# Attention ends in another order, norm chains by halves, and merged products whose bank halves VectorE adds

## The chip, the cores and the metric

One Trainium2 chip; the program runs on 1 of its cores. The metric is the device time of one execution in microseconds (us), and the median of the runs shown is taken.

## What is computed

Two transformer blocks over 256 tokens of width 1024, in float32, as a chain of ten stages on one residual x:

```python
# layer 0: neighborhood attention; layer 1: differential attention
x = x + rms_norm(attention(rms_norm(x, g0)), g1)
x = x + rms_norm(conv_glu_ffn(rms_norm(x, g2)), g3)     # gelu(conv3(h@Wg)+b) * (h@Wv) @ Wo, inner width 2816
x = x + sigmoid(rms_norm(x, g4) @ Wgate) * (p @ Wproj)  # "ple"
# second block, once
h = h + 0.5 * (silu(n(h)@Wg) * (n(h)@Wu)) @ Wd          # "glu", inner width 2816
h = h + mixer(n(h))                                     # HGRN2 and causal attention
h = h + 0.5 * (silu(n(h)@Wg) * (n(h)@Wu)) @ Wd
h = h + sigmoid(n(h) @ Wgate) * (p @ Wproj)
return rms_norm(h)
```

## The kernel before

`PHASES` (stages 0 to 9) is na, ffn, ple, da, ffn, ple, glu, mix, glu, ple. x lies as two tiles of 128 tokens by 1024.

**Products in three parts.** Each float32 product is made of three TensorE matmuls in the reduced format fp32r (`product3`, L1419 to L1421): high part by high part, low by high, high by low, summed in PSUM. Every weight slab of 128 x 2048 values is loaded into `raw` (3 slots), ScalarE copies it into `w_hi` (L615), VectorE subtracts the copy into `w_lo` (L953); both have `RING` = 5 slots. `feed(upto)` on either engine works through the slabs in order up to that number, and waits until the slot's last reader is done. The activations lie transposed in `hT_hi` and `hT_lo`, two separate tiles of 8 x 256 columns.

**PSUM.** Four banks `acc` of 512 columns, and four banks `work`, used in turn: group g opens bank g % 4 when group g-4 has been read out.

**Feed-forward stages (`ffn`).** 22 tiles c of 128 inner channels. `up(c)`: gate product into columns 0 to 255 of one bank, value product into columns 256 to 511 of the same, 8 k-steps of three 256-wide matmuls each. VectorE runs the convolution (three instructions, ffn only), ScalarE the gelu or silu, VectorE multiplies by the value half (L1204), ScalarE makes the high part (L789), VectorE the low part (L1209). `down(c)`: 12 matmuls of 512 columns into `acc`. TensorE's order is up(c), down(c-1). Even tiles carry three slab conversions on both engines.

**Attention (`attention`).** TensorE runs 16 groups of columns, c.0 to c.15 (`half_columns`: 8 k-steps of three 256-wide matmuls), which give transposed queries and keys; ScalarE reads each bank out (`columns_out`). `gap(ph, n)` lists what runs behind group n: S u (scores of head pair u), T u (transposition of its weights), V u (values), O q (transposition of half of the output). S u stands at `SCORED[u]`; T u 2 groups later in stage 0 and 3 in stage 3; V u one more. VectorE's `scores` scales, adds the table (L1058) and takes the maximum (L1063); ScalarE's `exps` follows, then in stage 3 VectorE's `weights` (L1068 to L1077). `tail(ph)` orders the rest: P are pieces of the output projection's first half, K of its second half; K (t, half) ends `acc` bank 2t + half.

**Ends of stages (`end_of_acc`, the end of `ffn`).** For each token tile: ScalarE's square sum over 1024 columns (L619), on the row of GpSimd mean and power (L501, L502), VectorE's two instructions that scale by gain and add to x (L1019, L1023; `post`), a second square sum (`pre`), mean and power again, VectorE's scaling (L1009; `normed`), TensorE's transposition (L1464; `turn_x`), and the parts of hT (`tile_parts`, L985, L624, L964). Between these stands one `feed`.

Of the kernel before, what the change touches and what calls it, by code (L numbers as in the profile page):

```python
# [20 lines left out]
ALU = mybir.AluOpType  # L21
# [43 lines left out]
SCORED = [3, 4, 7, 8, 11, 12, 15]  # L65
# [12 lines left out]
def tail(ph):  # L78

    first = [] if ph == 0 else [("V", 5)]  # L80
    return first + [("P", (0, 0)), ("S", 7), ("P", (0, 1)), ("T", 6), ("P", (1, 0)), ("V", 6), ("T", 7),
                    ("P", (1, 1)), ("V", 7), ("O", 1), ("K", (0, 0)), ("K", (0, 1)), ("K", (1, 0)), ("K", (1, 1))]


def plan(w):
# [47 lines left out]
    def event(name, n, scale, squares):  # L133
        E[name] = (len(ev), cols[0])
        cols[0] += n
        cols[1] += squares
        ev.append((n, scale, cols[1]))
# [5 lines left out]
    for t in range(T):  # L143
        event(f"pre0.{t}", 1, 1.0 / D, 1)
    for ph, kind in enumerate(PHASES):
# [48 lines left out]
        elif kind in ("ffn", "glu"):  # L194
            norm_stage(ph, 1)
            stage(f"up{ph}", FT - 1)
            if PHASES[ph + 1] == "ple":
                stage(f"pT{ph + 1}", 1, 1)
            stage(f"last_up{ph}", 1)
# [6 lines left out]
            B[f"down{ph}"] = count["down"]  # L206
            for j in range(STEPS):
                add(a[:, a0 + j * FB:a0 + (j + 1) * FB].rearrange("(k p) n -> p k n", p=P), KT, FB, "used")
                t_slab(b, b0 + j * FB, G[f"up{ph}"] + 2 * j + 1 if j < STEPS - 1 else G[f"last_up{ph}"])
                count["down"] += 2  # L210
                add(c[j * FB:(j + 1) * FB, :].rearrange("(k p) n -> p k n", p=P), 2, D,
                    ("down", count["down"]))
# [47 lines left out]
        for name in {"na": ("post0", "pre0", "post1", "pre1"), "da": ("post0", "pre0", "post1", "pre1"),  # L260
                     "ffn": ("post0", "post1", "pre0", "pre1")}.get(kind, ("pre0", "pre1")):
            event(f"{name[:-1]}{ph if name[:4] == 'post' else ph + 1}.{name[-1]}", 1, 1.0 / D, 1)
# [3 lines left out]
def two_blocks(nc, w, out):  # L266
# [3 lines left out]
    with ctx:  # L270
# [17 lines left out]
        hT_hi = sb("hT_hi", [P, KT, S], F32R)  # L288
        hT_lo = sb("hT_lo", [P, KT, S], F32R)
# [37 lines left out]
        cbuf, glu, hid32 = z(0, 512, (2, S)), z(512, 1024, (2, S)), z(1024, 1536, (2, S))  # L327
        pp, prow = z(2048, 4096, (T, D)), z(4096, 4608, (T, 256))
# [18 lines left out]
        ebr = z(9216, 9728, None, 8)  # L347
        tT = sb("tT", [8, 32])
# [24 lines left out]
        conv_done, act_done = sem("conv_done"), sem("act_done")  # L373
        hid_hi_done, hid_ready, sig_done = sem("hid_hi_done"), sem("hid_ready"), sem("sig_done")
# [28 lines left out]
        def up_bank(ph, c):  # L403
            return G[f"up{ph}"] + c if c < FT - 1 else G[f"last_up{ph}"]
# [10 lines left out]
        def score_bank(u):  # L415
            return 2 * (u % 2) if u < 6 else 2
# [43 lines left out]
        def _(sp):  # L460
# [9 lines left out]
            for t in range(T):  # L470
                sp.wait_ge(out_ready, t + 1)
                sp.dma_start(out[0, t * P:(t + 1) * P, :], xn[:, t, :]).then_inc(stored, 16)
            sp.wait_ge(stored, 16 * T)
# [3 lines left out]
        def _(pool):  # L477
# [18 lines left out]
            def powers(name):  # L496
                while raised[0] <= names.index(name):
                    i, c = E[names[raised[0]]]
                    n, scale, squares = EV[i]
                    pool.wait_ge(sq_done, squares)  # L500
                    link(pool.tensor_scalar(ms[:, c:c + n], ssq[:, c:c + n], scale, EPS, ALU.mult, ALU.add))  # L501
# [39 lines left out]
            pool.wait_ge(x_ready, 2)  # L541
# [63 lines left out]
        def _(act):  # L605
# [30 lines left out]
            def pre(ph, t):  # L636
                if ph == 0:
                    act.wait_ge(x_loaded[t], 16)
                else:
                    act.wait_ge(x_ready, 2 * (ph - 1) + t + 1)  # L640
                square_sum(xn[:, t, :], x[:, t, :], E[f"pre{ph}.{t}"][1])

            def post(ph, t):
                if ph in ACC:
                    act.wait_ge(acc_full, ACC[ph] + 2 * t + 2)
                else:
                    act.wait_ge(down_done, B[f"down{ph}"] + FT - 1 + t)
                square_sum(xn[:, t, :].rearrange("p (a b) -> p a b", a=2), acc[:, 2 * t:2 * t + 2, :],
                           E[f"post{ph}.{t}"][1])

            def end_of_acc(ph, b, finish):
                feed(b + 5)
                finish(0)
                feed(b + 6)
                pre(ph + 1, 0)
                tile_parts(ph + 1, 0)
                finish(1)
                feed(b + 7)
                pre(ph + 1, 1)
# [50 lines left out]
            def columns_out(ph, n):  # L710
                g, f = G[f"c{ph}.{n}"], n // 4 * 2 + n % 2
                if n // 2 % 2 == 0:
                    evac(g, backwards(qT[:, f, :].rearrange("p (t c) -> p t c", t=T)),
                         bank(g)[:, 0:S].rearrange("p (t c) -> p t c", t=T))
                else:
                    evac(g, kT[:, f, :], bank(g)[:, 0:S])

            def attention(ph):
# [8 lines left out]
                for n in range(HALVES):  # L727
# [3 lines left out]
                    columns_out(ph, n)  # L731
# [11 lines left out]
                if ph == 3:  # L743
                    for u in after(ph, gap(ph, HALVES - 1), "V") + [5]:
                        head_squares(ph, u)
                unit_exps(ph, 6)
                feed(wo + 5)
                unit_exps(ph, 7)
                weights_turned(ph, 6)
                if ph == 3:  # L750
                    head_squares(ph, 6)
                weights_turned(ph, 7)
                if ph == 3:
                    head_squares(ph, 7)
                output_parts(ph, 1)
# [13 lines left out]
            def ffn(ph, kind):  # L769
                b, c0 = B[ph], B[f"down{ph}"]  # L770
                feed(b + 3)
                for c in range(FT):
# [8 lines left out]
                    else:  # L781
                        full(act, g)
# [1082 lines left out]
```

## Time and profile before

| | |
|---|---|
| median of 3 runs | 1406.74 us (1406.55 to 1407.74) |
| the profiled execution | 1408.87 us |
| its span, first to last instruction | 1407.3 us |
| granted clock, mean | 0.955 |
| PE, PEld, DVE, ACT, POOL busy | 90%, 81%, 59%, 45%, 8% |

PE are TensorE's matmuls, PEld its weight loads, DVE is VectorE, ACT ScalarE, POOL GpSimd. A granted clock of 1.00 is 2.4 GHz, 0.50 is 1.2 GHz. The ends of matmuls are modelled, so the pace of TensorE is read from the distance of starts, not from durations. Where matmul follows matmul closely the profile calls PE busy, whatever the pace. The stages take, by the writes of x: 0 to 188 us na, to 386 ffn, to 416 ple, to 583 da, to 780 ffn, to 819 ple, to 1011 glu, to 1178 mix, to 1373 glu, to the end ple.

### The profile page before, as it was taken

To read this page: it belongs to the slowest core of one execution; us is meant where nothing else is said; L and a number is where in the kernel's file an instruction comes from. 1 tells how busy PE (TensorE), PEld (TensorE's weight loads), DVE (VectorE), ACT (ScalarE), POOL (GpSimd) and SP (SyncE) were. 2 spreads that over 40 slices of the span, in tenths; PEclk is the share of its full clock that TensorE was granted. 3 is DMA by queue.
4 is the path that set the end of the run, shared out by engine and by line. 5 is a ranking of instruction groups with operands and counts; after the bars stand their busy time and mean duration, and the time that the engine had idled before them with its cause. 6 is when DMAs were issued, how large, how long until landed. Compare 5 with 4: busy or idle time off the path is not lost. (4 is left out here: it accounts for less than half of the span.)

```text
span 1407.3 us, 19395 instructions
## 1 busy us (share of the span) xinstructions
PE 1264.3 (90%) x8145; PEld 1144.0 (81%) x8145; DVE 826.4 (59%) x921; ACT 629.0 (45%) x854; POOL 108.2 (8%) x216
## 2 busy tenths in 40 slices
PE   6997769999999776699999979999889987999997
PEld 5887669999878764599998779999767776999995
DVE  6645346666776654566666845555456775444455
ACT  5634334444465552344444644434354643333444
POOL 4000030000010000100000100000015321000000
PEclk9999889999999989899999989999999998999999
DMA  9631155555447320265554525555243324655550
GB/s 287 210 115 63 58 158 180 180 180 180 180 165 233 115 73 30 86 203 192 191 188 151 187 90 182 188 193 193 84 149 113 131 72 149 202 180 180 180 176 35
DMA packets 148730, 214.62 MB, mean 153 GB/s; under 512 B 4378, under 2 KB 114396, under 8 KB 148644
## 3 DMA queue, kind: packets, MB, share of 16 engines
q1 hardware_dynamic: 145356, 205.62, 43.9%
q0 software_dynamic: 1632, 4.71, 1.3%
q10 hardware_dynamic: 1656, 3.05, 0.6%
q8 instruction: 65, 1.06, 0.3%
q14 instruction: 21, 0.17, 0.0%
HBM read 212.30 MB, written 1.06 MB: 152 GB/s over the span
## 5 line engine op out<-in xcount | busy, mean ns | idle before, releaser
L953 DVE TENSOR_TENSOR w_lo<-raw,w_hi 128x2048 fp32r<-128x2048 f32 (+1 forms) x195 | 445.1, 2289 | 213.2 <-PE work L1421 131.2
L1419 PE MATMUL work<-hT_hi,w_hi 128*128 128x256 f32 x1696 | 488.7, 288 | 11.1 <-DVE hT_lo L964 6.1
L1420 PE MATMUL work<-hT_lo,w_hi 128*128 128x256 f32 x1696 | 485.6, 286 | 0.0
L1421 PE MATMUL work<-hT_hi,w_lo 128*128 128x256 f32 x1696 | 485.3, 286 | 0.0
L615 ACT ACTIVATE w_hi<-raw 128x2048 fp32r<-128x2048 f32 (+1 forms) x195 | 368.3, 1894 | 10.8 <-DMA raw<-in_na_w_qkv 9.4
L1419 PEld LDWEIGHTS work<-hT_hi,w_hi 128*128 128x128 f32 x1696 | 331.6, 195 | 19.8 <-issue 16.7
L1420 PEld LDWEIGHTS work<-hT_lo,w_hi 128*128 128x128 f32 x1696 | 331.5, 195 | 3.1
L1421 PEld LDWEIGHTS work<-hT_hi,w_lo 128*128 128x128 f32 x1696 | 331.1, 195 | 0.0
L1419 PE MATMUL acc<-w_hi,aux_hi 128*128 128x512 f32 x384 | 151.6, 395 | 6.5 <-DVE aux_lo L1209 3.6
L1420 PE MATMUL acc<-w_lo,aux_hi 128*128 128x512 f32 x384 | 150.5, 392 | 0.0
L1421 PE MATMUL acc<-w_hi,aux_lo 128*128 128x512 f32 x384 | 149.5, 389 | 0.0
L780 ACT ACTIVATE Z<-Z 128x256 f32<-128x256 f32 x44 | 18.4, 418 | 199.3 <-DVE Z L1199 199.3
L501 POOL TENSOR_SCALAR ms<-ssq 128x1 f32<-128x1 f32 (+2 forms) x38 | 17.4, 458 | 1156.7 <-ACT xn L619 1022.6
L783 ACT ACTIVATE Z<-work 128x256 f32<-128x256 f32 x44 | 16.9, 384 | 194.4 <-PE work L1421 194.4
L1419 PEld LDWEIGHTS acc<-w_hi,aux_hi 128*128 128x128 f32 x384 | 72.4, 189 | 21.6 <-issue 6.9
L666 ACT ACTIVATE Z<-work 128x512 f32<-128x512 f32 (+3 forms) x98 | 48.5, 515 | 92.4 <-PE work L1421 76.2
L1196 DVE TENSOR_SCALAR Z<-work,convT 128x256 f32<-128x256 f32 x44 | 23.8, 541 | 107.3 <-PE work L1421 107.3
L1421 PEld LDWEIGHTS acc<-w_hi,aux_lo 128*128 128x128 f32 x384 | 72.1, 188 | 15.8
L1419 PE MATMUL acc<-w_hi,hT_hi 128*128 128x512 f32 x176 | 74.5, 423 | 8.2 <-DVE hT_lo L964 7.8
L1420 PEld LDWEIGHTS acc<-w_lo,aux_hi 128*128 128x128 f32 x384 | 72.5, 189 | 11.6
L1204 DVE TENSOR_TENSOR Z<-Z,work 128x256 f32<-128x256 f32 x88 | 36.7, 418 | 63.2 <-ACT Z L783 51.6
L1464 PE MATMUL work<-ident,xn 128*128 128x128 f32 x112 | 23.4, 376 | 54.9 <-DVE xn L1009 54.5
(201 smaller groups left out, 1421.5 us busy)
## 6 DMA issues: line engine op xcount, KB each, us to landing
raw<-in_ffn_w_in SPq DMA_DIRECT2D x44, 1024.0 KB, 5.7
raw<-in_ffn_w_out SPq DMA_DIRECT2D x22, 1024.0 KB, 5.0
raw<-in_w_gate SPq DMA_DIRECT2D x22, 1024.0 KB, 5.4
raw<-in_w_up SPq DMA_DIRECT2D x22, 1024.0 KB, 5.8
raw<-in_w_down SPq DMA_DIRECT2D x22, 1024.0 KB, 4.9
raw<-in_na_w_qkv SPq DMA_DIRECT2D x12, 1024.0 KB, 6.7
raw<-in_da_w_qkv SPq DMA_DIRECT2D x12, 1024.0 KB, 5.3
raw<-in_ple_w_gate SPq DMA_DIRECT2D x8, 1024.0 KB, 5.1
```

The lines of the kernel that those rows point to most:

```text
L501: link(pool.tensor_scalar(ms[:, c:c + n], ssq[:, c:c + n], scale, EPS, ALU.mult, ALU.add))
L615: act.activation(w_hi[:, n % RING, 0:size], raw[:, n % RAW, 0:size], ACT.Copy).then_inc(hi_done, 1)
L666: act.activation(dst, src, func).then_inc(bank_free[g % WORK], 1)
L780: act.activation(glu[:, c % 2, :], cbuf[:, c % 2, :], ACT.Gelu_apprx_tanh).then_inc(act_done, 1)
L783: act.activation(glu[:, c % 2, :], bank(g)[:, 0:S], ACT.Silu).then_inc(act_done, 1)
L953: dve.tensor_tensor(w_lo[:, n % RING, 0:size], raw[:, n % RAW, 0:size], w_hi[:, n % RING, 0:size].bitcast(F32), ALU.subtract).then_inc(lo_ ...
L1196: link(dve.tensor_scalar(dst, src[:, 0:S], tap[1], tap[3], ALU.mult, ALU.add))
L1204: dve.tensor_tensor(hid32[:, c % 2, :], glu[:, c % 2, :], bank(g)[:, S:2 * S], ALU.mult)\
L1419: pe.matmul(dst, stationary[0], moving[0], start=first, stop=False)
L1420: pe.matmul(dst, stationary[0], moving[1], start=False, stop=False)
L1421: return pe.matmul(dst, stationary[1], moving[0], start=False, stop=last)
L1464: ins = pe.transpose(b[:, cols(i)], v[:, t, cols(4 * q + i)], ident[:, :])
```

## The change

1. **Merged products.** `hT_hi` and `hT_lo` become halves of one tile `hT_both` [P, 8, 2, 256]. In `up` and `half_columns` a k-step is one 512-wide matmul (w_hi by both parts, into both halves of a bank) and one 256-wide (w_lo by the high part, into the first half). Gate and value get a bank each, so a tile takes two groups instead of one. VectorE adds the halves of each bank with a `tensor_reduce` of 512 columns into 256.
2. **In ffn and glu** the convolution and the silu read the sum in SBUF (`gsum`), the value's sum goes to `hid32`, and the product is made in place. In **attention** the read-out of c.n moves from ScalarE to VectorE, at the head of each turn n of its loop.
3. **Norm chains by halves.** Square sums over 512 columns, two for each tile; GpSimd makes two mean steps and one power; `post` multiplies `acc` by the gain without waiting for the power, then scales and adds to x, one half at a time; x_ready, out_ready and down_done count halves.
4. **Attention ends.** S 6 moves from group 15 to 14. `tail` moves V 7 and O 1 ahead of P (1, 1) in stage 0 and V 7 ahead of it in stage 3. The transposition of x's first tile moves behind K (1, 1). In `end_of_acc` VectorE's `normed` moves ahead of its `feed(b + 6)`, and `feed(b + 7)` behind all parts; `feed(wo + 6)` moves into the attention.

```diff
-SCORED = [3, 4, 7, 8, 11, 12, 15]
+SCORED = [3, 4, 7, 8, 11, 12, 14]
...
+    late = {0: [("S", 7), ("P", (0, 0)), ("T", 6), ("P", (0, 1)), ("V", 6), ("T", 7), ("P", (1, 0)), ("V", 7), ("O", 1),
+                ("P", (1, 1))],
+            3: [("S", 7), ("P", (0, 0)), ("V", 5), ("P", (0, 1)), ("T", 6), ("P", (1, 0)), ("V", 6), ("T", 7), ("V", 7),
+                ("P", (1, 1)), ("O", 1)]}[ph]
+    return late + [("K", (0, 0)), ("K", (0, 1)), ("K", (1, 0)), ("K", (1, 1))]
...
-            stage(f"up{ph}", FT - 1)
+            stage(f"up{ph}", 2 * (FT - 1))
...
-        hT_hi = sb("hT_hi", [P, KT, S], F32R)
-        hT_lo = sb("hT_lo", [P, KT, S], F32R)
+        hT_both = sb("hT_both", [P, KT, 2, S], F32R)
+        hT_hi, hT_lo = hT_both[:, :, 0, :], hT_both[:, :, 1, :]
...
+                    if halves:
+                        pool.wait_ge(sq_done, squares - 1)
+                        link(pool.tensor_scalar(ms[:, c + 1:c + 2], ssq[:, c:c + 1], scale, EPS, ALU.mult, ALU.add))
+                        pool.wait_ge(sq_done, squares)
+                        link(pool.tensor_scalar(ms[:, c:c + 1], ssq[:, c + 1:c + 2], scale, ms[:, c + 1:c + 2],
+                                                ALU.mult, ALU.add))
...
+                for q in range(2):
+                    dve.wait_ge(sq_done, EV[i][2] - 1 + q)
+                    half = slice(q * 512, (q + 1) * 512)
+                    ins = dve.tensor_tensor(xn[:, t, half], acc[:, 2 * t + q, :], gb[:, half], ALU.mult)
+                link(ins)
+                dve.wait_ge(rstd_done, i + 1)
+                for q in range(2):
+                    half = slice(q * 512, (q + 1) * 512)
+                    dve.scalar_tensor_tensor(out=x[:, t, half], in0=xn[:, t, half], scalar=rstd[:, c:c + 1],
+                                             in1=x[:, t, half], op0=ALU.mult, op1=ALU.add).then_inc(x_ready, 1)
...
                 finish(0)
+                normed(ph + 1, 0)
                 feed(b + 6)
-                normed(ph + 1, 0)
                 tile_parts(ph + 1, 0)
                 finish(1)
-                feed(b + 7)
                 normed(ph + 1, 1)
                 if ph + 1 == 3:
                     feed(b + 8)
                 tile_parts(ph + 1, 1)
+                feed(b + 7)
...
+            def columns_out(ph, n):
+                g, f = G[f"c{ph}.{n}"], n // 4 * 2 + n % 2
+                full(dve, g)
+                if n // 2 % 2 == 0:
+                    dst, src = backwards(qT[:, f, :].rearrange("p (t c) -> p t c", t=T)), "p (e t c) -> p t c e"
+                    src = bank(g).rearrange(src, e=2, t=T)
+                else:
+                    dst, src = kT[:, f, :], bank(g).rearrange("p (e s) -> p s e", e=2)
+                dve.tensor_reduce(dst, src, AX.X, ALU.add).then_inc(bank_free[g % WORK], 1)
...
                 for n in range(HALVES):
                     ops = gap(ph, n - 1)
+                    columns_out(ph, n)
                     for u in after(ops, "S"):
                         scores(ph, u)
...
+                    src, hid = gsum[:, c % 2, :], hid32[:, c % 2, :]
+                    dve.tensor_reduce(src, bank(g).rearrange("p (e s) -> p s e", e=2), AX.X, ALU.add)\
+                        .then_inc(bank_free[g % WORK], 1)
...
+                    full(dve, g + 1)
+                    dve.tensor_reduce(hid, bank(g + 1).rearrange("p (e s) -> p s e", e=2), AX.X, ALU.add)\
+                        .then_inc(bank_free[(g + 1) % WORK], 1)
...
-                if kh == 1 and t == 1 and half == 0:
+                if kh == 1 and t == 1 and half == 1:
                     turn_x(ph + 1, 0)
...
+                            pe.matmul(b.rearrange("p (e s) -> p e s", e=2), v[0][:, k, cols(c % 2)], hT_both[:, k, :, :],
+                                      start=k == 0, stop=False)
+                            ins = pe.matmul(b[:, 0:S], v[1][:, k, cols(c % 2)], hT_hi[:, k, :],
+                                            start=False, stop=k == KT - 1)
```

## Rows read from the trace of the kernel before

**Rows 1.** The page: span, then busy time, share and instructions of each engine.
```profile
span 1407.3 us, 19395 instructions
...
PE 1264.3 (90%) x8145; PEld 1144.0 (81%) x8145; DVE 826.4 (59%) x921; ACT 629.0 (45%) x854; POOL 108.2 (8%) x216
```

**Rows 2.** Waits of PE: engine, line, releaser: total us, times, longest.
```profile
PE work L1464 <- DVE xn L1009: 54.5, 11, 8.3
PE work L1441 <- DVE Z L1077: 13.3, 7, 3.0
```

**Rows 3.** Timeline, PE, feed-forward stage: start us, us, engine line op tiles shape count.
```profile
861.09 0.39 PE L1421 MATMUL acc<-w_hi,aux_lo 128*128 128x512 f32 x1
861.32 0.28 PE L1419 MATMUL work<-hT_hi,w_hi 128*128 128x256 f32 x1
861.43 0.28 PE L1420 MATMUL work<-hT_lo,w_hi 128*128 128x256 f32 x1
861.55 0.28 PE L1421 MATMUL work<-hT_hi,w_lo 128*128 128x256 f32 x1
```

**Rows 4.** Timeline, DVE, two tiles of a feed-forward stage; in brackets idle before and releaser.
```profile
263.15 0.55 DVE L1196 TENSOR_SCALAR Z<-work,convT 128x256 f32<-128x256 f32 x1 [4.78 <-PE work L1421]
...
274.94 0.43 DVE L1209 TENSOR_TENSOR aux_lo<-Z,aux_hi 128x256 fp32r<-128x256 f32 x1 [0.54 <-ACT aux_hi L789]
280.15 0.54 DVE L1196 TENSOR_SCALAR Z<-work,convT 128x256 f32<-128x256 f32 x1 [4.78 <-PE work L1421]
```

**Rows 5.** Windows: stretch, busy us (count) of PE, PEld, DVE, ACT, POOL, clock, DMA, GB/s.
```profile
245.00:280.00 35.00, 35.00 (x251) 33.03 (x250) 22.10 (x26) 14.18 (x14) 0.00 (x0) 1.00 0.55 181
172.00:176.00 4.00, 4.00 (x12) 3.20 (x11) 2.29 (x4) 1.26 (x2) 0.00 (x0) 0.50 0.42 148
```

**Rows 6.** Groups by line and shape: count, busy us, mean ns, idle before and releasers.
```profile
L953 DVE TENSOR_TENSOR w_lo<-raw,w_hi 128x2048 fp32r<-128x2048 f32 x191 | 438.2, 2301 | 211.8 <-PE work L1421 131.2 <-ACT w_hi L615 80.6
...
L1204 DVE TENSOR_TENSOR Z<-Z,work 128x256 f32<-128x256 f32 x88 | 36.7, 418 | 63.2 <-ACT Z L783 51.6 <-ACT Z L780 11.6
...
L1063 DVE TENSOR_REDUCE stat<-Z 128x4 f32<-128x1024 f32 x16 | 19.5, 1220 | 0.6
```

**Rows 7.** Timeline, DVE, ACT and PE, loop of the first attention.
```profile
76.11 1.29 DVE L1058 SCALAR_TENSOR_TENSOR Z<-acc,Z 128x512 f32<-128x512 f32 x2 [4.07 <-PE acc L1549]
...
79.16 0.38 ACT L666 ACTIVATE Z<-work 128x256 f32<-128x256 f32 x1 [5.47 <-PE work L1421]
...
84.67 1.29 DVE L1058 SCALAR_TENSOR_TENSOR Z<-acc,Z 128x512 f32<-128x512 f32 x2
...
89.94 2.91 PE L1573 MATMUL work<-Z 128*128 128x64 f32 x16 [2.94 <-ACT Z L666]
```

**Rows 8.** Timeline, DVE and PE, loop of the second attention.
```profile
480.32 1.28 DVE L1058 SCALAR_TENSOR_TENSOR Z<-acc,Z 128x512 f32<-128x512 f32 x2
...
484.83 0.66 PE L1441 MATMUL work<-ident,Z 128*128 128x128 f32 x4 [1.92 <-DVE Z L1077]
```

**Rows 9.** Timeline, all engines, end of the first attention.
```profile
162.37 1.03 ACT L619 ACTIVATE xn<-acc 128x1024 f32<-128x1024 f32 x1 [7.43 <-PE acc L1421]
...
168.26 0.98 POOL L501 TENSOR_SCALAR ms<-ssq 128x1 f32<-128x1 f32 x1 [3.85 <-ACT xn L619]
...
170.46 1.97 PE L1464 MATMUL work<-ident,xn 128*128 128x128 f32 x8 [5.41 <-DVE xn L1009]
...
176.97 1.02 ACT L619 ACTIVATE xn<-acc 128x1024 f32<-128x1024 f32 x1 [3.10 <-PE acc L1421]
...
185.26 1.97 PE L1464 MATMUL work<-ident,xn 128*128 128x128 f32 x8 [8.32 <-DVE xn L1009]
```

**Rows 10.** Timeline, PE: first down of a feed-forward stage, end of the second gated stage.
```profile
203.35 0.47 PE L1419 MATMUL acc<-w_hi,aux_hi 128*128 128x512 f32 x1 [0.92 <-DVE aux_lo L1209]
...
803.97 1.85 PE L1464 MATMUL work<-ident,xn 128*128 128x128 f32 x8 [1.99 <-DVE xn L1009]
...
815.55 1.97 PE L1464 MATMUL work<-ident,xn 128*128 128x128 f32 x8 [6.11 <-DVE xn L1009]
```

More of the change, by code:

```diff
@@ L636, in pre @@
             def pre(ph, t):
[L637 to L641, printed above, removed]
-            def post(ph, t):
[L644 to L649, printed above, removed]
+                for q in range(2):
+                    if ph:
+                        act.wait_ge(x_ready, 4 * (ph - 1) + 2 * t + q + 1)
+                    elif q == 0:
+                        act.wait_ge(x_loaded[t], 16)
+                    half = slice(q * 512, (q + 1) * 512)
+                    square_sum(xn[:, t, half], x[:, t, half], E[f"pre{ph}.{t}"][1] + q)
+            def post(ph, t):
+                for q in range(2):
+                    if ph in ACC:
+                        act.wait_ge(acc_full, ACC[ph] + 2 * t + q + 1)
+                    else:
+                        act.wait_ge(down_done, B[f"down{ph}"] + FT - 1 + 2 * t + q)
+                    square_sum(junk[:, 2 * t + q, :], acc[:, 2 * t + q, :], E[f"post{ph}.{t}"][1] + q)
             def end_of_acc(ph, b, finish):
@@ L653, in end_of_acc @@
                 finish(0)
-                feed(b + 6)
+                feed(b + 7 if PHASES[ph] in ("na", "da") else b + 6)
                 pre(ph + 1, 0)
@@ L769, in ffn @@
             def ffn(ph, kind):
-                b, c0 = B[ph], B[f"down{ph}"]
+                b, c0, d0 = B[ph], B[f"tiles{ph}"], B[f"down{ph}"]
                 feed(b + 3)
@@ L781, in ffn @@
                     else:
-                        full(act, g)
-                        act.activation(glu[:, c % 2, :], bank(g)[:, 0:S], ACT.Silu).then_inc(act_done, 1)
+                        evacuated(act, g)
+                        act.activation(glu[:, c % 2, :], gsum[:, c % 2, :], ACT.Silu).then_inc(act_done, 1)
                     if c % 2 == 0:
@@ L1140, in attention @@
                     expand(7)
-                feed(wo + 5)
-                if ph == 3:
-                    weights(ph, 6)
                 scores(ph, 7)
@@ L1148, in attention @@
                 else:
+                    weights(ph, 6)
                     weights(ph, 7)
@@ L1151, in attention @@
                 output_parts(ph, 1)
+                feed(wo + 6)
             def attention7(base):
@@ L1184, in ffn @@
             def ffn(ph, kind):
-                b, c0 = B[ph], B[f"down{ph}"]
+                b, c0, d0 = B[ph], B[f"tiles{ph}"], B[f"down{ph}"]
                 layer = ph // 3
@@ L1410, in _ @@
                 dve.wait_ge(gb_loaded, 16 * 6)
-                dve.scalar_tensor_tensor(out=xn[:, t, :], in0=x[:, t, :], scalar=rstd[:, c:c + 1], in1=gb[:, :],
-                                         op0=ALU.mult, op1=ALU.mult).then_inc(out_ready, 1)
+                for q in range(2):
+                    half = slice(q * 512, (q + 1) * 512)
+                    dve.scalar_tensor_tensor(out=xn[:, t, half], in0=x[:, t, half], scalar=rstd[:, c:c + 1],
+                                             in1=gb[:, half], op0=ALU.mult, op1=ALU.mult).then_inc(out_ready, 1)
         @block.tensor
```

148 lines of the change are left out of this document (70 added, 78 removed).

## The prediction

> **What bounds the kernel now.** I read the page first. TensorE is busy for 1264.3 of the 1407.3 us, VectorE for 826.4, ScalarE for 629.0 [rows 1]. The windows of 35 us then part the span in two kinds of stretch. In the feed-forward stages (four, some 190 us each, over half of the span) TensorE is busy throughout at the full clock, VectorE for 22.1 of 35 us [rows 5]. There the pace of TensorE sets the end and nothing else does: VectorE ends two tiles with 4.78 us of idling [rows 4]. Elsewhere TensorE waits, and the list of its waits names for whom: 54.5 us in 11 waits for the scaled x in front of the transposition at an end of a stage, 13.3 us for the softmax weights of the second attention [rows 2]. Behind such a wait it runs for some us at the lower clock level, 0.50 of full, which is 1.2 GHz [rows 5].
>
> **Merged products.** A 256-wide matmul starts 0.12 us behind the one before it, a 512-wide one takes 0.23, and the first 256-wide one behind a 512-wide one took 0.11 [rows 3]. The 0.228 I take for a 512-wide one comes from the tiles: two take 280.15 - 263.15 = 17.00 us [rows 4], a tile's 48 narrow matmuls 48 x 0.12 = 5.76, its 12 wide ones the other 8.50 - 5.76 = 2.74. A k-step is now 3 x 0.12 = 0.360 us; merged it is 0.227 and then 0.113 to 0.12, so 0.340 to 0.347. Every narrow matmul now stands behind a wide one, which is the place of the 0.11, and I take 0.3405: 19.5 ns saved. The other end is 7 ns, with 0.233 for a wide one that is slowed by its narrow neighbours. There are 4 x 22 x 2 x 8 = 1408 such k-steps, some 48 of them at 1.2 GHz, where both forms need the time of their columns and nothing is saved: 1360 x 19.5 ns = **26.5 us** (ends 9.5 and 26.5). Two tiles then take 2 x (16 x 0.3405 + 2.74) = 16.4 us.
>
> The Trainium skill ("TensorE: Matmul & The Clock Gate", section "Wait — 56ns, not 53.3ns?") puts starts N / 2.4 GHz + 2.5 ns apart, 109 and 216 ns here. By it a merged k-step would be 325 ns; from the measured 360 that would be 35 ns, 48 us in all, but its 327 for three narrow ones isn't what rows 3 show.
>
> **What the merge adds.** VectorE sums 512 columns of a bank, twice a tile. The nearest row is the maximum over 1024 columns: 1.22 us for 1024 elements [rows 6]; with some 0.15 of it fixed, 512 elements are 0.68 us. Here the pairs lie 256 columns apart in PSUM, which no row shows; a second pass for each element would be 1.2 us. I take 0.68, keep 1.2 as an end, and leave out a gain, since no instruction goes but the 0.4 us read-outs of ScalarE. [...]
>
> Does VectorE stay under 16.4 us? I laid its order out against TensorE, 0 being the end of an even tile's gate product. Sum 0.7; convolution to 2.2; the value product ends at 2.7, its sum at 3.45; conversion 2.25 [rows 6], to 5.7; product 0.42 [rows 6], to 6.1; conversion to 8.3; low part 8.6; conversion to 10.8. The odd tile's gate ended at 8.2: its sum starts late, at 10.8, convolution to 12.9, sum to 13.6, product to 14.0, parts to 15.0. That is 1.4 us short of the next even gate, and both low parts come before their `down` (10.9 and 19.1). So the sums are hidden by VectorE's 4.78 us of idling; without that cover each 0.1 us on a sum costs 0.4 us for two tiles. A glu tile has no convolution. Banks: two groups a tile leave the bank of two tiles ago, long read.
>
> The first `down` of an ffn stage waited 0.92 us at 203.35 [rows 10], since the convolution began behind the whole first tile; the gate now ends 2.7 us sooner. Twice 1.0: **2.1 us**.
>
> **Attention loops: a cost.** VectorE now first waits for c.n and then does the scores. In stage 0 it did those of u = 2 at 76.11, right behind them; now they wait for c.8, which ended at 79.16 less a little, and for 0.7 of summing [rows 7]: start at 79.9. Behind follow 2.5 us of scores, 0.6 of output, 2.25 of conversion, 0.95 of table, the sum of c.9: the scores of u = 3 start at 86.6 and not at 84.67, and with them move its exponentials and the values that waited 2.94 us at 89.94 [rows 7]: 1.95 us. Queued behind the waiting VectorE are these scores and a conversion; TensorE waits for them at the values. The pair before it loses 1.7 by the same count. In stage 3 the scores of u = 3 started at 480.32 behind a conversion that waited for ScalarE [rows 8]; ScalarE, rid of the read-outs, gives it sooner, and the pairs lose 1.3 and twice 0.25. Stage 0: -3.65, stage 3: -1.8. The k-steps save 12 x 8 x 19.5 ns = 1.9 in front of the first waits, of which I take 1, as loads are dense in the first 70 us. Sum **-4.4 us**; with sums of 1.2 us some 8 more.
>
> **Attention ends.** Stage 0, counted from the end of the scores of u = 4 at 101.5 [rows 7]: the last column group moves from 22 to 25 us behind it, but scores 6 and O 1 lie ahead of pieces of the projection that cover their chains. By the same count the first K starts at 50.5, not at 53.5, and with no wait in front of it the four K run at the full clock, 11.0 us: the last ends at 61.5. Before, it ended at 75.4 (176.9), since x's first transposition stood ahead of it and waited 5.41 us, which set the clock to 0.50 [rows 5, 9]. Then comes the chain of the second tile, 8.3 us from 176.97 to 185.26 [rows 9]. By halves it gives 0.45 at each square sum (half of 1.03 is hidden), 1.1 at `post` (the gain product beside GpSimd's power), 0.8 at GpSimd's mean, which took 0.98 at 168.26 beside a VectorE conversion that is gone from there. But the first tile's parts now stand in front of it on both engines, so that it takes 10.4 us, to 71.9. The transposition before stood at 83.7: 11.8 saved. Stage 3 in the same way: K from 53.3 instead of 56.5, end at 66.3, transposition at 76.5 instead of 86.2: 9.7. Sum **21.5 us**; if O 1's cover fails, half.
>
> **Other ends.** End of stage 5: waits of 1.99 and 6.11 us at 803.97 and 815.55 [rows 10]. VectorE's moved conversion now delays the parts of the first tile by 1.5, the halves save 0.45 and 0.8 twice: 3.2 in all. In the same manner 0.8 at stage 2, 0.85 at 6, 1.5 at 7, 0.8 each at 1 and 4, 0.6 at the output: **8.5 us**.
>
> **Sum.** 26.5 + 2.1 - 4.4 + 21.5 + 8.5 = 54.2 us off the profiled span of 1407.3: 1353.1. The median of the runs lies 0.6 below that span (the profiled execution itself took 1408.87, 1.6 around it): 1352.5.
>
> **The rivals.**
> - *The merge saves little*: a k-step 353 ns, 17 us less: 1370. For it: no row shows wide and narrow in turn; against: the 0.11 in rows 3.
> - *VectorE bound in ffn*: a sum of 1.2 us adds 2.1 us to its 15.0 for two tiles; at about 16.9 the 22 pairs of ffn lose 11, the loops 8: 1371.
> - *The ends stay long*, because the in-order VectorE and ScalarE hold the second tile's chain behind the first's parts, or the clock falls once more in the loops: 11 us less: 1363.
> - *Slower than before*: the sum reads pairs 256 columns apart at a third of the pace or worse. Its place is VectorE's queue in ffn and the loops. 22 pairs of tiles at 4 sums each and 24 sums in the loops make 112 us for each us by which a sum exceeds 0.68, less the slack of 41: it eats the 54 from 1.5 us a sum; at 1.9 the time is 1450. Against it stands the pace of 1.2 ns an element in rows 6.
> - *Starts cost less once merged* (325 ns): 21 us more: 1332. It is the skill's rule of above; rows 3 have 0.23 and 0.11, not 0.216 and 0.109.
>
> **How the numbers follow.** Forecast 0.61 (1342 to 1364), merge 0.12, VectorE bound 0.10, ends 0.10, slower 0.05, starts 0.02. The range of 1338 to 1377 takes in all but the last two and half of the far ends. Faster 0.94, same 0.01, slower 0.05; 0.2% is about what this kernel's measurement can tell from no change.
>
> **What the profile would show.** Right: in ffn starts 0.34 us apart from k-step to k-step, the convolution's pairs every 16.4 us, VectorE's sums at 0.7 us and idle time left behind the odd tile; K pieces without a wait between them; one wait of about 9 us at each attention end where two of 5.4 and 8.3 stood; values in stage 0 waiting 4 us. Wrong: starts of 0.12 behind wide ones, TensorE waiting for aux_lo or for a bank in ffn, sums over 1 us, a wait at the end of the loops for the bank of O 0, or long stretches at 0.50.

## The result and the profile after

The changed kernel takes 1385.1 us (median of 4 runs, 1384.8 to 1385.6), the one before 1407.2 beside it: a ratio of 0.984, 95% interval 0.983 to 0.986. The change gains 22 us. The forecast was 1352.5 with a range of 1338 to 1377: the sign is right, the gain is two fifths of the 54 us, and the time lies outside the range.

The page of the kernel after, against [rows 1]:

```profile
span 1383.6 us, 16609 instructions
...
PE 1251.3 (90%) x6481; PEld 1051.3 (76%) x6481; DVE 955.4 (69%) x1153; ACT 627.7 (45%) x882; POOL 116.2 (8%) x246
```

TensorE issues 1664 matmuls fewer (one for each of the 1408 merged k-steps of the feed-forward stages and the 256 of the attention columns), but is busy for only 13 us less; VectorE took on 129 us. The waits of TensorE (in us: total, times, longest), against [rows 2]:

```profile
PE work L1498 <- DVE xn L1019: 41.4, 11, 8.4
PE work L1475 <- DVE Z L1090: 9.7, 5, 3.6
PE work L1608 <- ACT Z L683: 7.8, 3, 3.7
...
PE work L1608 <- DVE xn L1102: 7.1, 3, 4.4
```

The waits for the normed x fell from 54.5 to 41.4 us. The last row is as good as new: three waits of the values (L1608) for VectorE's read-out of an earlier output (L1102). Before, that wait came once, for 0.4 us.

To place the gain I cut both spans where the first product behind each stage starts. These are the first two cuts of before and then of after (timeline of PE: start, duration, instruction, idle time before it and its releaser):

```profile
188.76 0.55 PE L1419 MATMUL work<-hT_hi,w_hi 128*128 128x256 f32 x1 [1.53 <-DVE hT_lo L964]
389.00 0.50 PE L1419 MATMUL acc<-w_hi,hT_hi 128*128 128x512 f32 x1 [0.90 <-DVE hT_lo L964]
```

```profile
189.60 0.77 PE L1692 MATMUL work<-hT_both,w_hi 128*128 128x512 f32 x1 [1.53 <-DVE hT_both L974]
385.55 0.53 PE L1453 MATMUL acc<-w_hi,hT_both 128*128 128x512 f32 x1 [0.86 <-DVE hT_both L974]
```

| stage | before, us | after, us | measured | by the prediction's terms |
|---|---|---|---|---|
| 0 attention | 188.8 | 189.6 | +0.8 | -9.2 |
| 1, 4, 6, 8 feed-forward | 793.9 | 781.3 | -12.6 | -31.0 |
| 2, 5 | 64.1 | 60.4 | -3.6 | -4.0 |
| 3 attention | 166.4 | 159.6 | -6.8 | -7.9 |
| 7, 9 and output | 194.3 | 192.7 | -1.6 | -2.1 |

The last column sorts the terms of the forecast sum by stage (the 1 us from the loops' k-steps is counted in stage 0). Two cells carry the miss: 18 us in the feed-forward stages and 10 in stage 0. They have different causes.

**Feed-forward.** TensorE's timeline in the kernel after, three k-steps in the middle of stage 1, against [rows 3]:

```profile
299.88 0.40 PE L1692 MATMUL work<-hT_both,w_hi 128*128 128x512 f32 x1
300.11 0.28 PE L1694 MATMUL work<-hT_both,w_lo 128*128 128x256 f32 x1
300.23 0.40 PE L1692 MATMUL work<-hT_both,w_hi 128*128 128x512 f32 x1
300.46 0.28 PE L1694 MATMUL work<-hT_both,w_lo 128*128 128x256 f32 x1
300.57 0.40 PE L1692 MATMUL work<-hT_both,w_hi 128*128 128x512 f32 x1
300.82 0.28 PE L1694 MATMUL work<-hT_both,w_lo 128*128 128x256 f32 x1
300.94 0.40 PE L1692 MATMUL work<-hT_both,w_hi 128*128 128x512 f32 x1
```

Read the starts: from wide to wide 0.35, 0.34, 0.37 us. Over the 307 such steps between 200 and 380 us a wide matmul holds TensorE for 0.236 us and the narrow one behind it for 0.117: 353 ns a k-step. Over whole tiles it is 352.5, since the first wide matmul of a tile follows another wide one and mostly takes 0.227. VectorE over two tiles of the same stage, against [rows 4]:

```profile
242.07 0.69 DVE L1216 TENSOR_REDUCE Z<-work 128x256 f32<-128x512 f32 x1 [1.79 <-PE work L1694]
...
252.85 0.68 DVE L1216 TENSOR_REDUCE Z<-work 128x256 f32<-128x512 f32 x1
...
258.84 0.69 DVE L1216 TENSOR_REDUCE Z<-work 128x256 f32<-128x512 f32 x1 [1.78 <-PE work L1694]
```

Two tiles take 258.84 - 242.07 = 16.77 us (17.00 before). The sum is 0.69 us, the odd tile's starts late and without idling, and VectorE still idles for 1.78 us in front of the even one. So VectorE hides its new work, as laid out in the prediction; TensorE's own pace is what fell short.

**Stage 0.** VectorE in the loop of the kernel after, against [rows 7]:

```profile
83.63 0.69 DVE L1135 TENSOR_REDUCE Z<-work 128x256 f32<-128x512 f32 x1 [5.26 <-PE work L1573]
84.24 1.28 DVE L1071 SCALAR_TENSOR_TENSOR Z<-acc,Z 128x512 f32<-128x512 f32 x2
```

The sum of c.8 (L1135) stands ahead of the scores of u = 2 (L1071) in VectorE's queue. VectorE idles there for 5.26 us until TensorE ends c.8, and the scores wait with it, although TensorE had issued their products at 79.48. What TensorE meets for that in the loop and at its end (the row of 79.48 is that of the scores' products, the others are waits):

```profile
67.45 3.65 PE L1608 MATMUL work<-Z 128*128 128x64 f32 x16 [3.21 <-ACT Z L683]
77.55 2.00 PE L1608 MATMUL work<-Z 128*128 128x64 f32 x16 [1.32 <-DVE xn L1102]
79.48 1.13 PE L1584 MATMUL acc<-Z 64*128 64x256 f32 x8
...
96.16 3.65 PE L1608 MATMUL work<-Z 128*128 128x64 f32 x16 [3.75 <-ACT Z L683]
105.59 2.00 PE L1608 MATMUL work<-Z 128*128 128x64 f32 x16 [1.33 <-DVE xn L1102]
...
140.65 3.68 PE L1608 MATMUL work<-Z 128*128 128x64 f32 x16 [4.45 <-DVE xn L1102]
```

and the clock behind three of these waits (windows: stretch, busy us and count of PE, PEld, DVE, ACT, POOL, then the granted clock):

```profile
67.00:72.00 5.00, 4.54 (x22) 4.58 (x23) 2.29 (x1) 2.59 (x3) 0.00 (x0) 0.52 0.00 0
96.00:100.00 4.00, 3.84 (x18) 3.87 (x19) 1.67 (x1) 2.30 (x3) 0.00 (x0) 0.50 0.58 113
140.00:145.00 5.00, 4.36 (x20) 4.15 (x22) 1.21 (x6) 2.08 (x8) 0.00 (x0) 0.50 0.11 41
```

The last wait, 4.45 us, is new. The values of u = 5 need the bank that output(4) reads, and VectorE comes to it late:

```profile
136.92 0.68 DVE L1135 TENSOR_REDUCE Z<-work 128x256 f32<-128x512 f32 x1
137.52 1.28 DVE L1071 SCALAR_TENSOR_TENSOR Z<-acc,Z 128x512 f32<-128x512 f32 x2
138.83 1.22 DVE L1076 TENSOR_REDUCE stat<-Z 128x4 f32<-128x1024 f32 x1
139.96 0.17 DVE L1099 RECIPROCAL rinv<-rsum 128x4 f32<-128x4 f32 x1
140.17 0.42 DVE L1102 TENSOR_TENSOR xn<-work,rinv 128x256 f32<-128x256 f32 x1
```

In front of it stand the sum of c.15 and the scores of u = 6, which the change moved into the same gap (`SCORED`, 15 to 14). The end of the stage itself has the form that was forecast, one long wait in place of two, against [rows 9]:

```profile
176.96 1.09 PE L1498 MATMUL work<-ident,xn 128*128 128x128 f32 x8 [0.33 <-DVE xn L1019]
...
186.10 1.97 PE L1498 MATMUL work<-ident,xn 128*128 128x128 f32 x8 [8.05 <-DVE xn L1019]
```

### The profile page after: what moved, and what is told of

It is laid out like the page before. It is cut to its first block and busy times, and to the rows that moved or that the text cites. A ratio compares the mean times of both kernels' runs of the same rounds, so it can differ in the third digit from the quotient of the medians.

```text
span 1383.6 us, 16609 instructions
## 1 busy us (share of the span) xinstructions
PE 1251.3 (90%) x6481; PEld 1051.3 (76%) x6481; DVE 955.4 (69%) x1153; ACT 627.7 (45%) x882; POOL 116.2 (8%) x246
## 5 line engine op out<-in xcount | busy, mean ns | idle before, releaser
L1692 PE MATMUL work<-hT_both,w_hi 128*128 128x512 f32 x1408 | 509.7, 404 | 6.1 <-DVE hT_both L974 6.1
L1694 PE MATMUL work<-hT_both,w_lo 128*128 128x256 f32 x1408 | 399.2, 283 | 0.0
L1692 PEld LDWEIGHTS work<-hT_both,w_hi 128*128 128x128 f32 x1408 | 269.3, 191 | 73.5 <-issue 7.6
L1694 PEld LDWEIGHTS work<-hT_both,w_lo 128*128 128x128 f32 x1408 | 270.5, 192 | 3.0
L1216 DVE TENSOR_REDUCE Z<-work 128x256 f32<-128x512 f32 x88 | 60.4, 686 | 107.1 <-PE work L1694 107.1
L1230 DVE TENSOR_REDUCE Z<-work 128x256 f32<-128x512 f32 x88 | 60.4, 687 | 67.4 <-PE work L1694 67.2
L1571 PE MATMUL work<-hT_both,w_hi 128*128 128x512 f32 x256 | 98.6, 424 | 4.5 <-ACT Z L683 4.5
L799 ACT ACTIVATE aux_hi<-Z 128x256 fp32r<-128x256 f32 x88 | 36.9, 419 | 137.7 <-DVE Z L1236 137.7
L510 POOL TENSOR_SCALAR ms<-ssq 128x1 f32<-128x1 f32 x30 | 12.0, 399 | 953.4 <-ACT xn L634 495.9
L790 ACT ACTIVATE Z<-Z 128x256 f32<-128x256 f32 x44 | 18.4, 418 | 160.4 <-DVE Z L1225 160.4
L1454 PEld LDWEIGHTS acc<-w_lo,aux_hi 128*128 128x128 f32 x384 | 72.6, 189 | 11.8
L793 ACT ACTIVATE Z<-Z 128x256 f32<-128x256 f32 x44 | 18.4, 418 | 127.6 <-DVE Z L1216 127.6
L1453 PE MATMUL acc<-w_hi,hT_both 128*128 128x512 f32 x176 | 70.0, 398 | 6.1 <-DVE hT_both L974 6.0
L1573 PE MATMUL work<-hT_both,w_lo 128*128 128x256 f32 x256 | 74.0, 289 | 0.0
L1455 PE MATMUL acc<-w_hi,hT_both 128*128 128x512 f32 x176 | 68.6, 390 | 0.0
```

The source lines that it names most:

```text
L799: act.activation(aux_hi[:, c % 2, :], hid32[:, c % 2, :], ACT.Copy).then_inc(hid_hi_done, 1)
L1216: dve.tensor_reduce(src, bank(g).rearrange("p (e s) -> p s e", e=2), AX.X, ALU.add)\
L1230: dve.tensor_reduce(hid, bank(g + 1).rearrange("p (e s) -> p s e", e=2), AX.X, ALU.add)\
L1453: pe.matmul(dst, stationary[0], moving[0], start=first, stop=False)
L1454: pe.matmul(dst, stationary[0], moving[1], start=False, stop=False)
L1455: return pe.matmul(dst, stationary[1], moving[0], start=False, stop=last)
```

## The experiments

The theory: the feed-forward stages lack their gain because a merged k-step saves TensorE only 7 ns; the attention stages lack it because the sum of a column tile stands ahead of scores and outputs in VectorE's in-order queue. The rivals: the 0.69 us sums themselves cost, wherever they stand; the rearranged attention ends and the halves gain less than counted.

"After" is the changed kernel at 1385.1 us. It was not timed again beside the experiments. The kernel before was, and took 1408.9 to 1409.9 us there, against 1407.2 beside the change. So a difference from 1385.1 is sure only to 2 or 3 us, and the smaller ones below are also read from the traces. Stage 0 itself moves a little from trace to trace: with the same code in it, stage 1 starts at 189.6 us in after, 190.4 in e3, 188.4 in e4 and 190.8 in e10.

**e1_noqk: the attention columns without the merge.**

```diff
-  pe.matmul(b.rearrange(...), v[0][:, k, cols(n % 2)], hT_both[:, k, :, :], ...)
-  ins = pe.matmul(b[:, 0:S], v[1][:, k, cols(n % 2)], hT_hi[:, k, :], ...)
+  ins = product3(b[:, 0:S], both(v, every, k, cols(n % 2)), both(hT, every, k, every), ...)
-  columns_out(ph, n)      # VectorE
+  evac(g, ...)            # ScalarE, as before the change
```

> The changed kernel with one part undone: the query/key products are three narrow matmuls a k-step again and ScalarE reads their banks out. Theory A, VectorE's sums at the head of each turn of the attention loop cost more than the merge gives there: the first attention stage falls from 189.6 us by 8 to 12 (its loop lost 7.1 and its end some 8 by a wait of 4.45 us at 140.65 and the low clock behind it), the second changes by less than 3: 1373 to 1379 us. Theory B, the reordered ends (scores 6 in group 14) cost it: the wait of the values of u = 5 stays, at most 4 us are gained: 1381 to 1386.

Measured: 1366.7 us, ratio 0.970 (0.968 to 0.972). That is 18 us faster than the change and lies below both expectations: the merge of the query and key products makes this kernel slower. The last add to x in stage 0 ends at 172.0 us (183.5 after), and stage 3 is 4.2 us shorter. One wait remains that the kernel before doesn't have, in front of the values of u = 5, so it is not the sum's alone:

```profile
129.88 1.44 PE L1612 MATMUL work<-Z 128*128 128x64 f32 x6 [2.99 <-DVE xn L1108]
```

**e2_scores_first: the merge kept, the scores ahead of the sum.**

```diff
+  for u in after(ops, "S"):
+      scores(ph, u)
   columns_out(ph, n)
-  for u in after(ops, "S"):
-      scores(ph, u)
```

> The changed kernel, but VectorE does the scores of the group before ahead of the sum of c.n. Theory A1, the wait for c.n in front of the scores is the cost, not the 0.69 us of the sum: the scores of u = 2 start right behind S 2 again, the wait of V 2 falls from 3.75 us to under 3, and the whole gains 4 to 8 us: 1377 to 1381. Theory A2, it is the sum's own time and what else is queued: within 2 us of 1385.

Measured: 1368.7 us, ratio 0.972 (0.970 to 0.973), 16 us faster than the change with the same instructions, and more than the 4 to 8 us expected. So place, not work, costs most. Stage 3 is 10.3 us shorter than after, stage 0 only 4.5: there the outputs still stand behind the sum, and the wait of 4.67 us for L1102 is still there, at 135.87.

**e3_flat: the pattern of the wide matmul.** In place of two runs of 256 columns the moving operand and the bank are given as one run of 512.

```diff
-  pe.matmul(b.rearrange("p (e s) -> p e s", e=2), v[0][...], hT_both[:, k, :, :], ...)
+  pe.matmul(b, v[0][...], hT_both[:, k, :, :].rearrange("p e s -> p (e s)"), ...)
```

> The changed kernel, but the wide matmul of up is written with flat 512-column access patterns and not with two of 256. Theory P, the two-part pattern makes a wide matmul take 232 to 241 ns in place of 227: two tiles fall from 16.77 to about 16.5 us, 12 us in all: 1373. Theory Q, it is the turn of wide and narrow ones: no change, 1384 to 1386.

Measured: 1385.2 us, ratio 0.984: no change. The 353 ns don't come from the access pattern.

**e4_grouped: eight wide matmuls of a bank, then its eight narrow ones.**

```diff
   for k in range(KT):
       pe.matmul(... wide ...)
+  for k in range(KT):
       ins = pe.matmul(... narrow ...)
```

> The changed kernel, but in up the 8 wide matmuls of a bank come first and then its 8 narrow ones. Theory Q, a wide one costs 227 ns among wide ones and a narrow one 120 among narrow ones, and the change from one to the other costs the rest: a k-step falls from 0.353 to 0.347 us, two tiles from 16.77 to 16.55, 44 pairs by 0.2 us: 1376. Theory P, the pattern costs: wide ones stay at 232 and more, narrow at 120, no gain: 1385 or more.

Measured: 1377.8 us, ratio 0.978 (0.977 to 0.979): 7.3 us off, with the same matmuls in another order. Between 200 and 380 us a wide one now takes 0.229 us on average and a narrow one 0.119, so 348 ns a k-step against 352.5.

**e5_turn_back: the moved transposition put back.**

```diff
-  if kh == 1 and t == 1 and half == 1:
+  if kh == 1 and t == 1 and half == 0:
       turn_x(ph + 1, 0)
```

> Undoes one edit of the change: in the last product piece of both attention stages the transposition of x for the next stage is issued after half 0 of token tile 1 again, as in the kernel before, not after half 1. The prediction's attention-end term rests on it in part (the turn of tile 0 no longer in front of the last K piece). In the trace after the turn of tile 0 waits 0.33 us and the following one 8.05 us. If the move itself is worth something, the last K piece is delayed by the turn's wait on the normed x and each attention end is 2 to 6 us longer (time 1389 to 1397). If the end is bounded by the chain behind the last K piece and the halves already give the gain, the time stays at 1385 (+-1).

Measured: 1391.3 us, 6.2 more than after. The end of stage 0 in this kernel:

```profile
179.02 1.97 PE L1498 MATMUL work<-ident,xn 128*128 128x128 f32 x8 [3.04 <-DVE xn L1019]
...
190.21 1.97 PE L1498 MATMUL work<-ident,xn 128*128 128x128 f32 x8 [5.94 <-DVE xn L1019]
```

Both waits are back, though shorter than before. From the values of u = 5 (142.63 here, 140.65 after) to the second transposition it is 47.6 us, against 45.45: 2.1 us at this end, and 2.2 at that of stage 3 by the same count. The other 2 us lie in front of these stretches, where the edit changes nothing that I could name; stage 0 differs by as much between traces with the same code. So the move is worth some 4 us, not shown to be 6.

**e6_full_width: squares, means, gains and adds over 1024 columns again.**

```diff
-  for q in range(2):
-      act.wait_ge(acc_full, ACC[ph] + 2 * t + q + 1)
-      square_sum(junk[:, 2 * t + q, :], acc[:, 2 * t + q, :], ... + q)
+  act.wait_ge(acc_full, ACC[ph] + 2 * t + 2)
+  square_sum(xn[:, t, :].rearrange("p (a b) -> p a b", a=2), acc[:, 2 * t:2 * t + 2, :], ...)
...
```

> Undoes one part of the change: squares, means, gains, residual adds and the output's DMAs go by full 1024 columns of a token tile again, as in the kernel before; everything else of the change stays. The prediction put some 8.5 us on ends outside attention and a part of the 21.5 us of the attention ends on the halves. If that was right, this costs 10 to 16 us (time 1395 to 1401). Rival: what gains there is at the stage ends comes from the merged products and the moved turn, and the added instructions (two of half width for one) take back what the earlier start gives: then it stays within 3 us of 1385.

Measured: 1393.7 us, 8.5 more than after, below the 10 to 16 us expected. Measured against the kernel before beside it (1409.9) it is 6. The same stretch in front of the second transposition is 48.1 us at stage 0, 2.6 above after, and also 2.6 at stage 3: 5.2 us of it are at the two attention ends.

**e7_combo: the three findings together.** Stage 0 as in e1, stage 3 as in e2, products grouped as in e4 (the query and key products of stage 3 too).

> Three findings together: stage 0 (NA) keeps its three narrow products and ScalarE's read-out; stage 3 (DA) is merged with VectorE's scores ahead of its sum; in all merged products the eight wide matmuls of a bank come first and then the eight narrow ones. If the three gains add: stage 0 gives back 11.5 us (as its x ended 172.0 against 183.5 with three narrow products), stage 3 10 (140.0 against 150.3), grouping 7.5: 1385 less 29 is 1356. If the attention stages' gains with and without the merge come from the same waits, or grouping makes VectorE's sums late at the end of each bank, 1362 to 1368.

Measured: 1356.9 us, ratio 0.963 (0.962 to 0.964). The gains add: 1356 was expected.

**e8_combo_output_first: e7, and the outputs ahead of the scores.**

```diff
+  if ph == 0:
+      for u in after(ops, "V"):
+          output(u)
   for u in after(ops, "S"):
       scores(ph, u)
...
-  if ph == 0:
-      for u in after(ops, "V"):
-          output(u)
```

> As e7_combo, with one more edit: in both attention loops VectorE reads out the outputs V of a gap ahead of the scores S of that gap (as TensorE issues them). It tells what the wait at V5 is (3.0 us in e1_noqk at 129.9, 4.5 us in after at 140.65, both behind the read-out of V4, which stands behind scores 6 in VectorE's queue). If VectorE's queue order is the cause, that wait goes to under 1 us and the kernel is 2 to 4 us faster than e7_combo; if S6 in gap 14 itself is the cause (TensorE simply arrives early), the wait moves to the next scores and the times are within 1 us of each other.

Measured: 1350.4 us, ratio 0.958 (0.957 to 0.960), 6.5 below e7, where 2 to 4 had been expected. Of the wait 0.26 us is left, and the low clock is gone with the rest. First e7, then e8, the value matmuls of u = 5 and the window around them:

```profile
129.17 3.67 PE L1622 MATMUL work<-Z 128*128 128x64 f32 x16 [3.00 <-DVE xn L1109]
...
128.00:136.00 8.00, 6.83 (x27) 5.69 (x28) 3.56 (x8) 2.08 (x8) 0.00 (x0) 0.57 0.17 67
```

```profile
127.73 2.00 PE L1622 MATMUL work<-Z 128*128 128x64 f32 x16 [0.26 <-DVE xn L1109]
...
128.00:136.00 8.00, 8.00 (x51) 6.75 (x51) 6.06 (x10) 3.80 (x13) 0.00 (x0) 1.00 0.31 123
```

The same sixteen matmuls took 3.67 us at the low clock and 2.00 at the full one. A wait of 3.0 us cost stage 0 4.5 us (the last add to x at 171.1 and 166.6). The other 2 us of the difference are not in this wait; 1.6 of them lie in stage 3, whose code is the same.

**e9_split_wide: the merge undone on TensorE alone.** The sums stay on VectorE.

```diff
-  pe.matmul(b.rearrange(...), v[0][:, k, ...], hT_both[:, k, :, :], start=k == 0, stop=False)
+  if k == 0:
+      pe.matmul(... wide, as it was ...)
+  else:
+      for e, hT_e in enumerate((hT_hi, hT_lo)):
+          pe.matmul(b[:, cols(e, S)], v[0][:, k, ...], hT_e[:, k, :], start=False, stop=False)
```

> The changed kernel with every wide matmul (but the first of a bank, which opens it) as two narrow ones into the same two halves of the bank; VectorE still adds the halves, so nothing but TensorE's instructions differs. It measures the term of the sum that was 26.5 us in the prediction. 7 of 8 k-steps are split: 1232 of 1408. If a merged k-step saves 7 to 8 ns, as read from the trace after (352.8 ns against 360), the time is 8 to 10 us above 1385: 1394. If it saves the 19.5 ns of the prediction, 24 us: 1409. If TensorE's own pace isn't what ends the stages, it stays at 1385.

Measured: 1393.9 us, 8.8 above after. Besides the 1232 k-steps of the expectation, 224 of the attention stages are split. If all of them count it is 8.8 / 1456 = 6.0 ns each, if only the feed-forward's do 7.1; the starts in its trace (358.5 ns a k-step over whole tiles between 200 and 380 us, 14 of 16 split, against 352.5) say 6.9, and its four feed-forward stages, 7.2 us longer than after, say 5.9. For 1360 k-steps that is **8 to 10 us, where the sum had 26.5**.

**e10_pairs: wide, wide, narrow, narrow.**

```diff
   pe.matmul(... wide k ...)
-  ins = pe.matmul(... narrow k ...)
+  if k % 2:
+      for m in (k - 1, k):
+          ins = pe.matmul(... narrow m ...)
```

> In the merged up products two wide matmuls and then their two narrow ones (wide, wide, narrow, narrow) in place of wide, narrow, wide, narrow. e4_grouped (eight wide, then eight narrow) took 7.4 us off. If each change of width costs (about 10 ns for a wide matmul behind a narrow one), half of the changes go and about half of the gain is there: 1381 (+-1). If what counts is that a wide matmul's weights load beside a wide one (226 ns) and not beside a narrow one (113 ns), it is the same half. If it is a thing of the order of accumulation within the bank, it stays at 1385 or goes all the way to 1378.

Measured: 1379.0 us, ratio 0.978 (0.977 to 0.980). That lies between the two expectations, but the traces decide: from the first product to the last add to x, the four feed-forward stages take 8.8 us less than after in e10 and 7.9 less in e4. With half of the changes of width all of e4's gain is there, which a fixed price for each change doesn't give:

```profile
299.18 0.63 PE L1692 MATMUL work<-hT_both,w_hi 128*128 128x512 f32 x2
299.64 0.40 PE L1696 MATMUL work<-hT_both,w_lo 128*128 128x256 f32 x2
299.88 0.63 PE L1692 MATMUL work<-hT_both,w_hi 128*128 128x512 f32 x2
300.35 0.39 PE L1696 MATMUL work<-hT_both,w_lo 128*128 128x256 f32 x2
300.57 0.62 PE L1692 MATMUL work<-hT_both,w_hi 128*128 128x512 f32 x2
```

Two k-steps take 0.70 and 0.69 us, 348 ns each, and so it is over whole tiles (wide 0.233, narrow 0.115 on average).

**e11_all_merged: everything merged and grouped, VectorE's order V, S, sum.**

> All products merged (stage 0 too), in groups of eight wide and eight narrow, with VectorE's order in both attention loops: outputs V, scores S, and the sum of the column tile last. Against e8_combo_output_first (1350.4) only stage 0 differs: merged, with VectorE adding the halves instead of ScalarE reading out. If the merge in stage 0 was spoiled by VectorE's order alone, stage 0 (x ends at 166.6 us there) is 1 to 2 us shorter and the time 1349. If the sum costs in any order, since at stage 0 VectorE's instructions (0.68 us of sum and the waits of scores for k columns) stand in the way of the scores, x ends at 170 to 174 and the time is 1354 to 1358.

Measured: 1350.8 us, ratio 0.959 (0.956 to 0.962), not to be told from e8, where stage 0 isn't merged. The four runs stand apart in pairs, 1347.4 and 1347.5, 1354.0 and 1354.7, so this holds to some 3 us. Within that, in the right order the merge costs stage 0 nothing, and it gains nothing there either.

**e12_order_only: the changed kernel, VectorE's order V, S, sum, nothing else.**

```diff
-  columns_out(ph, n)
-  for u in after(ops, "S"):
-      scores(ph, u)
   if ph == 0:
       for u in after(ops, "V"):
           output(u)
+  for u in after(ops, "S"):
+      scores(ph, u)
+  columns_out(ph, n)
```

> The changed kernel with one edit: in both attention loops VectorE does the outputs V of a gap first, then the scores S, and the sum of the column tile last (as in e11_all_merged, but with wide and narrow matmuls in turn as in the change). e11 was 1350.8, and grouping alone (e4) took 7.4 us off, so if the two add, 1358 (+-3): the order of three entries in VectorE's queue is then worth 27 us, all that stages 0 and 3 lacked to the forecast. If grouping and order share their gain, or the two gains of e2 (16.4) and e8 over e7 (6.4) don't add in the merged kernel, 1362 to 1368.

Measured: 1355.8 us (5 runs, 1355.2 to 1357.2), ratio 0.962 (0.961 to 0.964). **Three entries of VectorE's loop in another order are worth 29 us**, more than the whole change had brought. Stage 0 ends its last add to x at 164.4 us (183.5 after), stage 3 is 9.8 us shorter. VectorE in the loop of this kernel:

```profile
78.73 1.29 DVE L1071 SCALAR_TENSOR_TENSOR Z<-acc,Z 128x512 f32<-128x512 f32 x2 [0.58 <-PE acc L1584]
80.06 1.22 DVE L1076 TENSOR_REDUCE stat<-Z 128x4 f32<-128x1024 f32 x1
81.75 0.69 DVE L1135 TENSOR_REDUCE Z<-work 128x256 f32<-128x512 f32 x1 [0.47 <-PE work L1573]
```

The scores start as TensorE delivers them and the sum comes behind, without a long idle time in front of either. TensorE's waits in this kernel, against those of after:

```profile
PE work L1498 <- DVE xn L1019: 41.2, 11, 8.3
...
PE work L1608 <- ACT Z L683: 5.7, 3, 3.4
PE work L1475 <- DVE Z L1090: 4.3, 2, 3.0
```

## Why the prediction was wrong

*The merged k-step: the term was mis-sized.* The prediction gave two ends, 7 ns and 19.5 ns, and took 19.5 because [rows 3] show one narrow matmul 0.11 us behind a wide one. The row holds nearly: narrow ones behind wide ones take 0.117 here, not 0.113. But the wide one behind a narrow one takes 0.236 and not 0.227, the "slowed by its narrow neighbours" of the other end. The number came from the transition at the edge of a run, and the merged form consists of transitions both ways. e9 measures 5.9 to 7.1 ns. Some 17 of the 32 missing us are this term; it is the first rival (353 ns), to which the prediction gave 0.12.

The Trainium skill ("TensorE: Matmul & The Clock Gate", section "Wait — 56ns, not 53.3ns?") would put the step at 325 ns. No order of these matmuls came near it: 353 ns in turn, 348 in pairs and in groups.

*VectorE's new work: right.* Sum 0.68 forecast, 0.69 measured; 15.0 us of VectorE's time for two tiles forecast, 16.77 - 1.78 = 15.0 measured. The rival of a VectorE bound fell, and that of slow pairs in PSUM with it. The wait of the first `down` is gone, as counted.

*The attention loops: the mechanism was right, the bill too short.* The prediction had the scores of u = 2 behind the sum of c.8, 3.8 us late, and named what is queued there. It priced one delay for each of two pairs, 1.7 and 1.95 us, 3.65 for stage 0. Counted from one even pair's scores on VectorE to the next, before 54.7, 76.1, 101.6 and after 56.1, 84.2, 112.3 us, the two periods grew by 6.7 and 2.6 us: 9.3, where the sum had 3.65. Two things were left out. The outputs V stand behind the same sum, which gives the two waits of 1.3 us; and behind the longer waits TensorE ran at 0.50. How the 9.3 part between them was not measured.

*The end of the loop: missed.* That the scores of u = 6, moved to gap 14, push the read-out of output(4) behind them, and with it TensorE's bank, stood in the diff and was not followed. The prediction looked for a wait "for the bank of O 0" and checked S 6 for its own chain, not for what is queued behind it. It is 4.45 us and again a stretch at half clock. e8 against e7 is the test: 4.5 us in stage 0 when the outputs go first.

*The ends of the attention stages: right in form.* The K pieces run without a wait, and one wait of 8.05 us stands where two of 5.4 and 8.3 stood. From the scores of u = 4 the last transposition was forecast 11.8 us nearer (83.7 to 71.9). In e12, where the loop no longer disturbs it, these scores start at 99.4 us and the transposition at 167.01: 67.6, even 4 us nearer than forecast. In the kernel after it is 73.8 (112.3 to 186.10), 9.8 us nearer than before with the wait of 4.45 in it, but these scores start 10.7 us later than before: the delay of the loop ate it. e5 gives the moved transposition 2.1 us of that and e6 the halves 2.6, where the prediction's pieces for halves (twice 0.45, 1.1, 0.8) make 2.8.

*Stage 3: the number is near by errors that cancel.* -7.9 was forecast, -6.8 measured. From the stage's first product to its first scores it takes 41.9 us against 37.1, which the forecast hadn't at all. 2.66 of these 4.9 us are a wait that the kernel before doesn't have there:

```profile
419.51 0.50 PE L1453 MATMUL work<-w_hi,hT_both 128*128 128x512 f32 x1 [2.66 <-DVE w_lo L963]
```

The change moved VectorE's conversions at this stage end; that this is the cause is read, not tested. The scores from u = 0 to u = 4 take 3.0 us more (forecast 1.8), and from there to the last transposition it takes 71.4 us against 86.1, 14.6 less (forecast 9.7). e2 and e12 show that some 10 us more were lost to VectorE's order.

*The other ends: near.* Stages 2 and 5 have -3.6 against -4.0, but as 1.7 and 1.9 where 0.8 and 3.2 were forecast (the pieces named for the 3.2, twice 0.45 and 0.8 less 1.5, don't add up to it). Stages 7, 9 and the output have -1.6 against -2.1.

The kernel with the mended order, 1355.8, lies 3.3 us above the forecast, but not for the forecast's reasons: the merge still lacks some 17 us there, and the attention stages give 18.3 and 16.6 us over before, where 9.2 and 7.9 had been forecast. That the total comes so near is luck. I had taken the loops of the kernel before as the best that they could be. What exactly in them became shorter (ScalarE without its read-outs is one candidate, the difference between e1 and e12 another) was only read from the traces, not taken apart.

## What to carry over

A read-out that waits for the newest product belongs behind all work whose input is already there: on an in-order engine the order of three entries, a 0.7 us sum the foremost, cost 29 us (e12), while the sum's execution cost nothing that e11 against e8 could show. When a diff moves an entry of such a queue, follow every bank and buffer that the entries *behind* it free, not only the moved entry's own chain. And a matmul's price is to be taken from a run of the same mixture; where the trace has only the edge of one, keep the whole interval as the forecast, or group equal widths.

## What the runs showed of the hardware

Three orders of the same matmuls, with 512 and 256 columns, at the full clock: in turn 352.5 ns for a k-step (353 within a run), two by two 348, eight by eight 348; as three narrow ones 360. The access pattern of the wide one makes no difference (e3). Why pairs already bring the whole gain stays open; a fixed price for each change of width doesn't explain it.

The sum of two bank halves, 256 results from pairs 256 columns apart in PSUM, takes 0.69 us. The prediction had scaled 0.68 from 1.22 us for 1024 neighbouring ones [rows 6], so no cost of the distance shows.

GpSimd's 128x1 mean took 0.98 us beside a VectorE conversion in [rows 9]. In e6 the same mean, the second of the first token tile, has the full-width form but no conversion beside it:

```profile
177.16 0.19 POOL L514 TENSOR_SCALAR ms<-ssq 128x1 f32<-128x1 f32 x1 [3.85 <-ACT xn L632]
```

A wait of TensorE costs more than its length: 3.0 us were 4.5 in e7 against e8, since the sixteen matmuls behind it took 3.67 us and not 2.00.
